# A three-part reordering of TensorE's small products in the two mixers of a four-layer network

## What is computed

```python
h = rms_norm_2(x, norm_mix_pre[l])
z = h @ w_in[l]
za, zq, zkv, zg, zc, zd = jnp.split(z, offsets, axis=-1)
y_conv = conformer_conv(za, ...)
y_nsa = nsa_attention(q, kv[:, :, 0], ..., gates, ...)
y_sgu = spatial_gating(zc, ...)
y_pool = multiscale_pool(zd, pool_w[l], pool_scale[l])
y = jnp.concatenate([y_conv, y_nsa, y_sgu, y_pool], axis=-1) @ w_out[l]
x = x + rms_norm_2(y, norm_mix_post[l])
```

```python
# compression, inside nsa_attention: 15 blocks of 32 tokens x 64 features
blocks = (t[:, blk_idx] + pe).reshape(bsz, n_cmp, CMP_LEN * HEAD_DIM)
return jax.nn.gelu(blocks @ w1) @ w2
# value products, 4 heads: probabilities times values in three branches
o = g[..., 0:1] * o_cmp + g[..., 1:2] * o_slc + g[..., 2:3] * o_win
# gating: 128x128 causal weights of 4 groups on 2 chunks of 128 tokens
f = jnp.einsum('gts,bcsgd->bctgd', ws, vr) + b_s.T[:, :, None]
```

## Time and profile before

| what | value |
|---|---|
| median of 3 runs | 1901.08 us |
| the three runs | 1901.0, 1903.31, 1901.08 us |
| span of the profiled execution | 1901.7 us |
| TensorE busy | 1805.5 us, 95% of the span |
| VectorE busy | 1466.5 us, 77% |
| ScalarE busy | 1049.8 us, 55% |
| GpSimd busy | 131.0 us, 7% |
| HBM read | 379.90 MB, 200 GB/s over the span |

### The profile page before, as it was taken

The page is one execution under the profiler, slowest core; times in us unless marked ns, Lnnn a source line. Parts: engine busy times, 40 slices in busy tenths (PEclk is TensorE's granted clock), DMA queues, the critical chain, the costliest instruction groups (busy, mean ns, idle before and its releaser), DMA issues.

```text
span 1901.7 us, 28364 instructions
## 1 busy us (share of the span) xinstructions
PE 1805.5 (95%) x9730; PEld 1512.8 (80%) x9730; DVE 1466.5 (77%) x2300; ACT 1049.8 (55%) x1594; POOL 131.0 (7%) x170
## 2 busy tenths in 40 slices
PE   5999899899999999999999999999889998979998
PEld 4888677688888887788878798878678887768886
DVE  6888788688888888868665576658869976878994
ACT  5554465465536553555454465545676645666663
POOL 1101010000010000000000000000012200002210
PEclk9999999899999999999999999999999999999999
DMA  9878665367888777444540164545145554324553
GB/s 384 339 274 313 236 232 210 113 220 277 279 305 287 276 278 271 165 179 176 180 151 1 64 243 176 194 177 193 67 180 191 184 194 160 112 89 169 185 193 117
DMA packets 63778, 382.04 MB, mean 201 GB/s; under 512 B 7153, under 2 KB 7409, under 8 KB 27586
## 3 DMA queue, kind: packets, MB, share of 16 engines
q1 hardware_dynamic: 42912, 300.96, 43.9%
q0 software_dynamic: 20208, 78.79, 11.5%
q10 hardware_dynamic: 578, 1.22, 0.2%
HBM read 379.90 MB, written 1.05 MB: 200 GB/s over the span
## 4 chain that ended last, share of the span: by engine, by line
PE 74%; DVE 14%; issue 6%; ACT 4%; DVEq 1%; DMA 1%; SPq 0%; ACTq 0%
PE ps L561 18%; PE ps L478 11%; PE ps L480 10%; PE ps L479 10%; PE ps L563 9%; DVE ring_lo L1615 3%; DVE wb L1914 2%; PE ps L843 1%; PE ps L582 1%; PE ps L584 1%; PE ps L583 1%; PE ps L609 1%; PE ps L869 1%; DVE wa L1903 1%; PE ps L856 1%
## 5 line engine op out<-in xcount | busy, mean ns | idle before, releaser
L1615 DVE TENSOR_TENSOR ring_lo<-ring,w_hi 128x1024 fp32r<-128x1024 f32 x534 | 666.5, 1265 | 257.5 <-ACT w_hi L1137 255.8
L1137 ACT ACTIVATE w_hi<-ring 128x1024 fp32r<-128x1024 f32 x556 | 579.1, 1057 | 458.7 <-PE ps L480 282.2
L561 PE MATMUL ps<-h_both,w_hi 128*128 128x512 f32 x1984 | 698.5, 397 | 0.0
L563 PE MATMUL ps<-h_both,ring_lo 128*128 128x256 f32 x1984 | 557.3, 281 | 0.0
L561 PEld LDWEIGHTS ps<-h_both,w_hi 128*128 128x128 f32 x1984 | 373.1, 188 | 89.0
L563 PEld LDWEIGHTS ps<-h_both,ring_lo 128*128 128x128 f32 x1984 | 375.8, 189 | 0.0
L478 PE MATMUL ps<-w_hi,h_both 128*128 128x512 f32 x580 | 236.8, 408 | 12.5 <-DVE h_both L2099 6.4
L480 PE MATMUL ps<-w_hi,h_both 128*128 128x512 f32 x580 | 230.2, 397 | 0.0
L479 PE MATMUL ps<-ring_lo,h_both 128*128 128x512 f32 x580 | 230.1, 397 | 0.0
L478 PE MATMUL ps<-w_hi,hid_lo 128*128 128x512 f32 x456 | 180.3, 395 | 1.3 <-DVE ring_lo L1615 1.3
L480 PE MATMUL ps<-w_hi,hid_hi 128*128 128x512 f32 x456 | 177.6, 389 | 0.0
(11 more groups left out here) (362 smaller groups left out, 2161.7 us busy)
## 6 DMA issues: line engine op xcount, KB each, us to landing
ring<-in_stream SPq DMA_DIRECT2D x276, 1024.0 KB, 4.8
arena<-in_mod POOLq DMA_DIRECT2D x128, 512.0 KB, 5.6
arena<-in_mod SPq DMA_DIRECT2D x14, 512.0 KB, 13.4
gate<-in_wide POOLq DMA_DIRECT2D x3, 1536.0 KB, 10.3
arena<-in_nsaw POOLq DMA_DIRECT2D x2, 1072.0 KB, 8.7
ring<-in_stream SPq DMA_DIRECT2D x4, 512.0 KB, 14.9
arena<-in_konst POOLq DMA_DIRECT2D x1, 1295.5 KB, 8.4
arena<-in_mixw POOLq DMA_DIRECT2D x2, 576.0 KB, 9.6
```

The lines of the kernel that those rows point to most:

```text
L561: nc.tensor.matmul(ps[:, banks[b], :].rearrange("p (w t) -> p w t", w=2), hi, h_both[:, :, 2 * r + i, :], start=(r == 0 and i == 0), stop= ...
L563: mm = nc.tensor.matmul(ps[:, banks[b], T:2 * T], lo, h_hi[:, 2 * r + i, :], start=False, stop=(r == 3 and i == 1))
L1137: nc.scalar.activation(w_hi[:, q % SPLITS, :], ring[:, half % SLOTS, (q % 2) * QUARTER:(q % 2 + 1) * QUARTER], ACT.Copy).then_inc(w_hi_rea ...
L1615: v.tensor_tensor(ring_lo[:, slot, cs], ring[:, slot, cs], w_hi[:, q % SPLITS, :], ALU.subtract).then_inc(w_lo_ready, 1)
```

## The change

Three edits of TensorE's stream. `compress` is cut into four pieces of eight positions each (`compress(n)`), and piece n follows step n of the four steps of `part(2, 3)`; the semaphore waits stand before piece 0; `quarter_done` is raised by the last of the twelve matmuls, as before, which now stands behind three of the pieces. `values` takes a pair of heads and goes through their products in turn; for that there are two copy buffers, and it waits for the second head's copy. `gating` multiplies both token tiles in one matmul of 2x64 columns.

```diff
-        nsaT = hidT[:, 4508:5532]
+        nsaT = [hidT[:, 4508:5532], arena[:, a0 + MIX_W + NS1 + NS0:a0 + MIX_W + NS1 + NS0 + 1024]]
...
-            def quarter(q, it, per, lhs, out_of, first, last, ends=False):
+            def quarter(q, it, per, lhs, out_of, first, last, ends=False, between=None):
...
-                mm.then_inc(quarter_done, 1)
+                    if n == 3:
+                        mm.then_inc(quarter_done, 1)
+                    if between is not None:
+                        between(n)
...
-                def compress():
-                    pe.wait_ge(blk_ready, l + 1)
-                    pe.wait_ge(cv_ready, l + 1)
-                    for e in range(CMP_LEN):
+                def compress(n):
+
+                    if n == 0:
+                        pe.wait_ge(blk_ready, l + 1)
+                        pe.wait_ge(cv_ready, l + 1)
+                    for e in range(n * CMP_LEN // 4, (n + 1) * CMP_LEN // 4):
...
-                    for tt in range(NT):
-                        for g in range(4):
-                            mm = nc.tensor.matmul(ps[:, 6, tt * C2 + g * HD:tt * C2 + (g + 1) * HD], mixw[:, g * P:(g + 1) * P],
-                                                  vn[:, tt, g * HD:(g + 1) * HD], start=True, stop=True)
+                    for g in range(4):
+                        mm = nc.tensor.matmul(ps[:, 6, :].rearrange("p (t n) -> p t n", t=NT)[:, :, g * HD:(g + 1) * HD], mixw[:, g * P:(g + 1) * P],
+                                              vn[:, :, g * HD:(g + 1) * HD], start=True, stop=True)
...
-                def values(h):
-                    i = NH * l + h
-                    pe.wait_ge(npT_copied, i + 1)
+                def values(pair):
+
+                    pe.wait_ge(npT_copied, NH * l + 2 * pair + 2)
                     vs = lambda w, tile: dv[:, tile, C2 + w * HD:C2 + (w + 1) * HD]
-                    dst = ps[h % 2 * HD:(h % 2 + 1) * HD, 7, h // 2 * T:(h // 2 + 1) * T]
+                    dst = [ps[e * HD:(e + 1) * HD, 7, pair * T:(pair + 1) * T] for e in range(2)]
                     for w in range(2):
-                        nc.tensor.matmul(dst, vs(w, 0), nsaT[:, w * FW:w * FW + T], start=(w == 0), stop=False)
-                        nc.tensor.matmul(dst[:, P:T], vs(w, 1), nsaT[:, w * FW + T:(w + 1) * FW], start=False, stop=False)
-                    nc.tensor.matmul(dst, vc, nsaT[0:NCMP, 6 * P:8 * P], start=False, stop=True).then_inc(no_sum, 1)
+                        for e in range(2):
+                            nc.tensor.matmul(dst[e], vs(w, 0), nsaT[e][:, w * FW:w * FW + T], start=(w == 0), stop=False)
+                        for e in range(2):
+                            nc.tensor.matmul(dst[e][:, P:T], vs(w, 1), nsaT[e][:, w * FW + T:(w + 1) * FW], start=False, stop=False)
+                    for e in range(2):
+                        mm = nc.tensor.matmul(dst[e], vc, nsaT[e][0:NCMP, 6 * P:8 * P], start=False, stop=True)
+                    mm.then_inc(no_sum, 1)
...
-                part(2, 3, bD)
-                compress()
+                part(2, 3, bD, compress)
...
-                values(0)
                 turn_probs(1)
                 out_chunk(1)
-                values(1)
+                values(0)
                 turn_probs(2)
                 gating()
-                values(2)
                 turn_gating()
                 turn_probs(3)
                 pe.wait_ge(sgu_out, l + 1)
                 out_chunk(2)
-                values(3)
+                values(1)
...
-                act.wait_ge(no_sum, NH * (l + 1))
+                act.wait_ge(no_sum, 2 * (l + 1))
...
-                    if h >= 1:
-                        dve.wait_ge(no_sum, i)
-                    v.tensor_copy(nsaT[:, 0:768], psf[:, bA * 512:bA * 512 + 768])
-                    v.tensor_copy(nsaT[0:NCMP, 768:1024], ps[0:NCMP, bA + 1, C2:512]).then_inc(npT_copied, 1)
+                    if i >= 2:
+                        dve.wait_ge(no_sum, i // 2)
+                    v.tensor_copy(nsaT[h % 2][:, 0:768], psf[:, bA * 512:bA * 512 + 768])
+                    v.tensor_copy(nsaT[h % 2][0:NCMP, 768:1024], ps[0:NCMP, bA + 1, C2:512]).then_inc(npT_copied, 1)
```

More of the change, by code:

```diff
@@ L290, in build @@
         mixw = arena[:, a0:a0 + MIX_W]
-        assert a0 + MIX_W + 2 * T + 2 * P + 2 * NCMP <= ARENA, a0
+        assert a0 + MIX_W + 2 * T + 2 * P + 2 * NCMP + 1024 <= ARENA, a0
         hidT = arena
@@ L903, in mixer, with part @@
                 bA, bC, bD = MIX_BANKS[0:3]
-                def part(j, r, bank):
+                def part(j, r, bank, between=None):
                     if j == 0 and r == 0:
@@ L916, in part @@
                     quarter(q0 + 4 * j + r, None, 0, lhs, lambda i, tt: ps[:, bank + tt, :],
-                            lambda i: r == 0 and i == 0, lambda i: r == 3 and i == 1)
+                            lambda i: r == 0 and i == 0, lambda i: r == 3 and i == 1, between=between)
                 def turn_gated():
```

## The result

| what | before | after |
|---|---|---|
| median | 1901.83 us (4 runs, 1901.0 to 1903.31) | 1909.95 us (4 runs, 1908.4 to 1913.68) |
| ratio of after to before | | 1.0043, 95% interval 1.0029 to 1.0058 |
| span, mean granted clock of the profiled execution | 1901.7 us, 0.980 | 1906.7 us, 0.976 |
| TensorE, VectorE, ScalarE busy | 1805.5, 1466.5, 1049.8 us | 1804.2, 1466.6, 1050.1 us |

The change costs 8.1 us (0.43%), where +2.4 was forecast; 1909.95 us lies above the forecast range of 1898.5 to 1907.5. No engine does more work: busy times are the same within 1.3 us. The profiled execution of after took 1908.4 us by the clock of the runs, 1.7 more than its span, and its other runs show the same 1.7. So the profile of before, with a span of 1901.7, was an execution of about 1903.4 us, one of the slower ones.

What follows compares the result with a forecast made beforehand. TensorE held 74% of the chain, the bound changing piece by piece in the mixers. Terms +0.12 - 0.92 + 0 + 1.6 + 1.6 = +2.4 us gave 1904.1 on the profiled span, 1903.5 against the runs; range 1898.5 to 1907.5.

Steps and rivals of the forecast that it cites:

- round trip: Compression: entering small tiles and returning to 128x128 costs 0.30 us per further piece, 0.9 for three.
- the recovered quarter: Weight quarter behind the compression's transposes: its recovered clock is worth nothing, since TensorE then waits for ScalarE's GELU.
- I expect the clock to stay up through them: Compression pieces: alternating with three full matmuls of 0.68 us, they keep the full clock.
- three returns come on top: Compression: if pieces lose the clock, mixer 0's 1.12 us is not won and three returns add cost.
- rival 4: Compression: the pieces still lose the clock, about +1.5 us per mixer, 1906 us; chance 0.04.
- +0.12 forecast: Compression in pieces, both mixers together: -0.22 us in mixer 0 and +0.34 in mixer 1.
- Gating: Gating of both tiles at once: VectorE no longer waits before its product, -0.46 us per mixer, -0.92 in all.
- Pairs themselves: Value products of two heads: about 2.05 us, like one head, so 0 on the path.
- rival 3: Value products: column halves take turns, +2.0 us at four pairs, 1911.5 or 1908.3 us; chance 0.06.
- Emptied places: Before the first pair and at chunk 2: lost work lets the clock fall, +1.6 us at each place.
- the toss before the first pair: Wait before heads 0 and 1: a clock fall is a toss in each mixer, counted as +1.6 us once.
- Rival 2: Emptied places: long clock falls, one over pair, transposes and gating costing 3.3 us; +5.7 in all, 1906.8 us; chance 0.17.

Runs made afterwards that it cites:

- best_filled: Kernel before with compression in pieces, gating of both tiles at once, ScalarE's two GELUs earlier and four zero products per mixer: 1903.29 us, ratio 1.0008.
- pieces_alone: Kernel before with the compression in four pieces and nothing else: 1902.68 us, ratio 1.0008.
- Pairs alone: Kernel before with the value products of two heads in turn and nothing else: 1909.8 us, ratio 1.0036.
- the filled version: Kernel before with the value products in pairs, plus ten products per mixer with a tile of zeros in TensorE's waits: 1900.36 us, ratio 0.9996.
- pairs_gating: Kernel after without its compression pieces, so value products in pairs and gating of both tiles at once: 1907.39 us, ratio 1.0031 to before.

## Why the prediction was wrong, and where it was right

*Compression, the sizes: right.* A round trip was put at 0.30 us and took 0.29; mixer 1 was to lose 0.34, and its transposes ended 0.31 us later behind `turn_gated()` than before (23.20 against 22.89). That the recovered quarter is worth nothing because of the GELU held in mixer 1: TensorE waited 1.77 us for it. By the Trainium skill (TensorE: Matmul & The Clock Gate, Single matmul latency) two drains near 175 ns would make an estimated 0.35; this case's trace shows somewhat less, 0.29.

*Compression, the clock: wrong as a certainty.* "I expect the clock to stay up through them" held in eight of ten mixers and failed in best_filled's mixer 1 and in after's mixer 0, where "three returns come on top" of the old loss (rival 4). What was missed altogether is that the longer wait for the GELU can be followed by a fall, with the next quarter, which nothing covers, behind it: 1.6 us in mixer 1. The prediction named that wait as its cover and didn't ask what comes behind it. That the wait brings the fall is argued and not shown: it came behind two of five such waits. After's profile holds +3.55 us at this part, the median of pieces_alone +1.5 (interval -1.1 to +4.2), against +0.12 forecast. That it is more than zero is not shown, nor how much of the whole it carries.

*Gating: right in its mechanism.* VectorE's wait of 0.46 us is gone and chunk 2 starts 0.55 us earlier in the trace. The time, -0.92 forecast and -0.8 measured, has an interval of -2.7 to +1.3, so a gain is not shown.

*Pairs themselves: right.* 2.03 us for two heads at the full clock; the halves run at once, so rival 3 was wrong.

*Emptied places: the step that failed.* The term was two further short falls, +3.2 us. Pairs alone measure +6.8 us (4.4 to 9.5), and the filled version takes all of it away. Both the place and the size were off. Place: the toss before the first pair was priced like chunk 2, but that place alone costs 1.1 us (interval -1.1 to +3.4) and the other 5.1. Size: 1.6 us a fall came from chunk 2 of mixer 0 in before, where a fall ended in a full quarter of weights (3.3 us long). The falls in this stretch with both places emptied went on through products, transposes and waits that nothing hides, and lasted 3.4 to 20.5 us, five of the six over 6.5. Rival 2 named that mechanism, put its longest at 6.5 us and its price at 3.3, and so its time at 1906.8; the longest cost 5.6 (mixer 1 against mixer 0 of pairs_gating). Rival 2 with 5.6 in the place of 3.3 gives 1909.1, near what was measured, but that nearness is partly luck: the profile of after, at 1908.4 us, has no fall over 6.8 us in its mixers, and gets there by more falls, at the compression too.

*The profile taken as a usual execution: wrong.* It was taken to stand 0.6 above the median. By its own time it was some 1903.4 us, 2.3 above the other two runs shown; the medians of before in the later comparisons are 1900.9 to 1902.3. The forecast is a median plus a difference, so its number doesn't move by that; but mixer 0's fall at chunk 2 was booked as a loss that the kernel had anyway (1.6 us), while most mixers that kept the clock there took 94.6 to 95.4 us for the main stretch instead of 97.2 (0.6 of the difference lies at the compression, where that mixer's fall was the longer one).

## What to carry to other kernels

Work that stands in front of a wait costs nothing and may still earn its place: taken out of a stretch that is already patchy, it can cost the clock of everything behind it that is on the path. Price such a fall by the whole patchy stretch at half clock, not by the shortest fall in the trace, and test it with filling products, which settle in one comparison whether the clock or a wait is the cause. Where runs of one kernel spread over 10 us of 1900, read mechanisms from the profiles and prices from medians of many runs.

## What was not expected

- The lower clock lasted 17 and 20.5 us at a stretch while TensorE was busy 13.7 of 16.9 and 16.4 of 20.5 us; in before the longest one in a mixer's main stretch was 6.8.
- Two kernels that differ in nothing but useless work differ by 0.4%: ratios to before of 1.0036 and 0.9996 (pairs), 1.0043 and 1.0002 (the whole change).
- The two emptied places: 1.0006 and 1.0027 singly, 1.0036 together. By the profiles only both together brought falls at the first pair; from six mixers that is an observation and no rule.
- A loss removed early came back elsewhere: with the GELUs ahead a fall near 45 us (44.8 to 49.4) stood in all six mixers. Three others had it too, two of them behind a slow quarter; what sets its place was not tried.
